# Squares of seven chunks added on GpSimd, and one visit of TensorE in place of seven, in three projections

## The reference, cut to what matters

```python
def rmsnorm(x, g):                       # first block: of x + g1 * y_lat, ahead of the second mixture of experts
    xf = x.astype(jnp.float32)
    y = xf * lax.rsqrt(jnp.mean(xf * xf, axis=-1, keepdims=True) + EPS)
    return (y * g.astype(jnp.float32)).astype(x.dtype)
...
m = stick_breaking_attention(hn, ...)    # ends with  o @ w_o   (1024 x 1024)
x = x + rms_norm(m, norm_gains[0, 1])
...
m = dilated_attention(hn, ...)           # ends with  o @ w_o   (512 x 1024)
x = x + rms_norm(m, norm_gains[1, 1])
```

## Time and profile before

| | |
|---|---|
| median of 3 runs | 2281.8 us (2281.36 to 2284.24) |
| span of the profiled execution | 2283.8 us |
| own time of the profiled execution | no other time is given for it than its span |
| PE busy | 2138.7 us (94%) |
| DVE busy | 1295.8 us (57%) |
| ACT busy | 1031.5 us (45%) |
| POOL busy | 133.7 us (6%) |
| mean granted TensorE clock | 0.973 of full speed |

### The profile page before, as it was taken

The page is one execution under the profiler, slowest core; times in us unless marked ns, Lnnn a source line. Parts: engine busy times, 40 slices in busy tenths (PEclk is TensorE's granted clock), DMA queues, the critical chain, the costliest instruction groups (busy, mean ns, idle before and its releaser), DMA issues.

```text
span 2283.8 us, 31295 instructions
## 1 busy us (share of the span) xinstructions
PE 2138.7 (94%) x13216; PEld 1640.1 (72%) x13216; DVE 1295.8 (57%) x1837; ACT 1031.5 (45%) x1501; POOL 133.7 (6%) x112
## 2 busy tenths in 40 slices
PE   5979989999997998999889999998999998999997
PEld 4656654577765665777667888886877776888885
DVE  3567765666637775355536766435255546766533
ACT  3556641255625664377744433324333355433331
POOL 0011200000001210000010000003000002000000
PEclk9989999999997998999999999999999999999998
DMA  9999970022217984211012222221222112222210
GB/s 398 384 361 370 369 298 0 17 95 112 112 75 263 357 343 187 111 38 38 38 74 111 105 80 111 92 110 52 91 95 95 48 71 78 111 77 108 111 56 37
DMA packets 40571, 324.12 MB, mean 142 GB/s; under 512 B 7231, under 2 KB 8255, under 8 KB 21695
## 3 DMA queue, kind: packets, MB, share of 16 engines
q1 hardware_dynamic: 27288, 288.91, 32.8%
q0 software_dynamic: 10624, 25.71, 3.2%
q10 hardware_dynamic: 2512, 7.41, 0.8%
HBM read 310.40 MB, written 24.19 MB: 147 GB/s over the span
## 4 chain that ended last, share of the span: by engine, by line
PE 85%; DVE 7%; ACT 4%; DMA 2%; issue 2%; POOL 0%; SPq 0%; DVEq 0%; ACTq 0%; POOLq 0%
PE PS L163 80%; PE PS L891 2%; PE PS L641 1%; DVE work L2344 1%; ACT work L1591 1%; DMA work<-tokens,slots 1%; PE PS L1152 1%; DVE WR L2350 1%; ACT XH L1284 0%; ACT work L1596 0%; ACT L1596 0%; DMA work<-in_xtok 0%; ACT work L1587 0%; DVE work L2405 0%; DMA ring<-in_wexp 0%
## 5 line engine op out<-in xcount | busy, mean ns | idle before, releaser
L163 PE MATMUL PS<-HS,RS 128*128 128x512 f32 x4128 | 951.0, 391 | 9.4 <-DVE HS L2121 8.6
L163 PEld LDWEIGHTS PS<-HS,RS 128*128 128x128 f32 x4128 | 773.8, 188 | 175.3 <-issue 13.7
L1765 DVE TENSOR_TENSOR RS<-ring,RS 128x1024 fp32r<-128x1024 f32 x212 | 259.0, 1224 | 342.2 <-ACT RS L1248 342.2
L1248 ACT ACTIVATE RS<-ring 128x1024 fp32r<-128x1024 f32 x212 | 221.5, 1052 | 252.3 <-PE PS L163 252.3
L1688 ACT ACTIVATE work<-work,vec 128x512 f32<-128x512 f32 x88 | 71.9, 817 | 239.5 <-DVE work L2471 239.5
L1765 DVE TENSOR_TENSOR CR<-ring,WR 128x1024 fp32r<-128x1024 f32 x128 | 153.3, 1222 | 37.5 <-ACT WR L1248 35.0
L163 PE MATMUL PS<-work 128*64 128x128 f32 (+5 forms) x1728 | 131.9, 294 | 29.7 <-DVE work L1824 19.9
L1248 ACT ACTIVATE WR<-ring 128x1024 fp32r<-128x1024 f32 x128 | 134.8, 1058 | 51.3 <-PE PS L163 44.9
L163 PEld LDWEIGHTS PS<-work 128*64 128x64 f32 (+2 forms) x1728 | 107.7, 147 | 49.4 <-issue 31.0
L1248 ACT ACTIVATE work<-PS 128x384 f32<-128x384 f32 (+2 forms) x194 | 86.7, 484 | 116.2 <-PE PS L674 37.4
L163 PE MATMUL PS<-RS,HS 128*128 128x512 f32 x480 | 116.0, 400 | 8.3 <-DVE HS L2121 8.3
(11 more groups left out here) (256 smaller groups left out, 2793.1 us busy)
## 6 DMA issues: line engine op xcount, KB each, us to landing
ring<-in_wexp SPq DMA_DIRECT2D x32, 2048.0 KB, 10.6
ring<-in_wmod SPq DMA_DIRECT2D x24, 2048.0 KB, 11.2
ring<-in_ffnu SPq DMA_DIRECT2D x22, 2048.0 KB, 8.1
ring<-in_wexp SPq DMA_DIRECT2D x32, 1024.0 KB, 11.0
ring<-in_ffnd SPq DMA_DIRECT2D x10, 2048.0 KB, 7.2
ring<-in_dilqk SPq DMA_DIRECT2D x6, 2048.0 KB, 8.1
ring<-in_sbqk SPq DMA_DIRECT2D x4, 2048.0 KB, 8.0
ring<-in_dilv SPq DMA_DIRECT2D x3, 2048.0 KB, 8.0
```

What stands on the lines that cost most here:

```text
L163: return T.matmul(out, l, r, start=start, stop=stop, skip_group_check=True)
L1248: return S.activation(out, x, ACT.Copy, **kw)
L1765: V.tensor_tensor(lo, src, hi.bitcast(F32), ALU.subtract).then_inc(w_lo, 1)
```

## The change

In calls 6, 8 and 12, ScalarE writes the square of chunk 0 to slot 0 of `sq`, those of chunks 1 to 7 in turn to slots 1, 2, 3 (`summed_square`, `summed_slot`). GpSimd adds the squares of chunks 1 to 6 to slot 0, one 128x512 add for each (`sum_squares`, semaphore `st_sum`). TensorE no longer visits the squares between the chunks: behind chunk 7's products `stat_sum` multiplies slot 0, once its six adds are done, and then the square of chunk 7. ScalarE waits with the square of chunks 4 to 7 for the add that read its slot before. `sum_squares(6)` is put ahead of `moe(1, 4)` in GpSimd's queue, `sum_squares(8)` ahead of the first `add_normed`, `sum_squares(12)` behind the fetches. The semaphore of the Abs is merged into that of the Exp.

```diff
--- before.py
+++ after.py
@@ -175,7 +175,8 @@
     ld_tab, tab_out, out_done = sem("landed_tables"), sem("tables_stored"), sem("out_stored")
     sc_ready = sem("sc_ready")
     ad_rows, ad_copy, ad_turn, ad_mod, ad_aff, ad_q = [sem("ada_" + n) for n in ("rows", "copied", "turned", "mod", "affine", "quarter")]
-    sq_act, sq_dve, st_add, st_sqrt, st_rcp, st_bc = [sem("stat_" + n) for n in ("sq_act", "sq_dve", "added", "sqrt", "rcp", "spread")]
+    sq_act, sq_dve, st_add, st_sum, st_sqrt, st_rcp, st_bc = [sem("stat_" + n) for n in (
+        "sq_act", "sq_dve", "added", "summed", "sqrt", "rcp", "spread")]
     md_a, md_b = sem("mod_scaled"), sem("mod_shifted")
     pl_mm, pl_ma, pl_md, pl_y, pl_x = [sem("pool_" + n) for n in ("means", "means_act", "means_dve", "product", "x")]
     rt_lg, rt_lt, rt_tr, rt_exp, rt_m, rt_rk, rt_blk = [sem("route_" + n) for n in ("logits", "biased", "turned", "exp", "chosen", "rank", "blocks")]
@@ -200,8 +201,8 @@
     nm_h, nm_l, rb_c, rc_c = sem("rows_hi"), sem("rows_lo"), sem("stat_row_copied"), sem("stat_column")
     pr_c, po_c = sem("rows_copied"), sem("out_copied")
     an_t, an_xp, an_xd = sem("add_scaled"), sem("add_pool"), sem("add_dve")
-    sk_q, sk_k, sk_z, sk_aa, sk_ad, sk_e, sk_ln, sk_s, sk_h, sk_l, sk_c, sk_t, sk_v = [sem("stick_" + n) for n in (
-        "q", "k", "z", "abs_act", "abs_dve", "exp", "log", "sum", "hi", "lo", "cumulated", "a", "values")]
+    sk_q, sk_k, sk_z, sk_ad, sk_e, sk_ln, sk_s, sk_h, sk_l, sk_c, sk_t, sk_v = [sem("stick_" + n) for n in (
+        "q", "k", "z", "abs_dve", "abs_exp", "log", "sum", "hi", "lo", "cumulated", "a", "values")]
     dq, dk, dz = sem("dil_q"), sem("dil_k"), [sem(f"dil_bias{i}") for i in range(3)]
     fu_r, fu_a, fu_d, fu_s, fu_f, fx_h, fx_l, fd_ca = [sem("ffn_" + n) for n in ("scaled", "tap2", "taps", "silu", "f", "f_hi", "f_lo", "copied_act")]
     po_half, own = sem("out_chunk"), sem("dve_step")
@@ -223,6 +224,11 @@
                 else:
                     na += 1
                     SQ[call, c] = (sq_act, na)
+    SUMMED = (6, 8, 12)
+
+    def summed_slot(c):
+        return (c - 1) % 3 + 1 if c else 0
+
     MD = (0, 16, 32, 48)
     BEFORE = [max([k for k in range(i) if CALLS[k][0] == CALLS[i][0]], default=-1) for i in range(len(CALLS))]
 
@@ -478,6 +484,16 @@
             for j in range(n // 128):
                 x = mm(PS[32 * j:32 * j + 32, s, 0:128], C("mean"), sq[:, i, j * 128:(j + 1) * 128], c == 0, c == 7)
             x.then_inc(st_add, 1)
+
+        def stat_sum(call):
+
+            s, n, both = CALLS[call]
+            for c, ready in ((0, (st_sum, 6 * SUMMED.index(call) + 6)), (7, SQ[call, 7])):
+                pe.wait_ge(*ready)
+                for j in range(n // 128):
+                    x = mm(PS[32 * j:32 * j + 32, s, 0:128], C("mean"), sq[:, summed_slot(c), j * 128:(j + 1) * 128],
+                           c == 0, c == 7)
+            x.then_inc(st_add, 8)
 
         def stat_spread(call):
             s, n, both = CALLS[call]
@@ -945,9 +961,7 @@
                     pe.wait_ge(f_l, k + 1)
                     x = mm3(PS[:, 4 + c % 2, :], (hi[:, k, :], lo[:, k, :]), hs(k), k == 0, k == 7)
                 x.then_inc(w_done, 1)
-                if c:
-                    stat_add(6, c - 1)
-            stat_add(6, 7)
+            stat_sum(6)
             stat_spread(6)
 
         def spread_sums(p, b, rl, at):
@@ -1010,9 +1024,7 @@
                 pe.wait_ge(po_c, po + c - 1)
                 x = out_products(first, kc, src_of, base, c, banks[c], range(0 if c else made, kc))
                 x.then_inc(w_done if c % per == per - 1 else po_half, 1)
-                if c:
-                    stat_add(call, c - 1)
-            stat_add(call, 7)
+            stat_sum(call)
             stat_spread(call)
 
         def stick():
@@ -1266,6 +1278,12 @@
             act.wait_ge(ready, value)
             S.activation(sq[:, SEQ[call, c] % 4, 0:x.shape[-1]], x, ACT.Square).then_inc(sq_act, 1)
 
+        def summed_square(call, c, x):
+            act.wait_ge(st_add, SEQ[call, 0])
+            if c > 3:
+                act.wait_ge(st_sum, 6 * SUMMED.index(call) + c - 3)
+            S.activation(sq[:, summed_slot(c), 0:x.shape[-1]], x, ACT.Square).then_inc(sq_act, 1)
+
         def table(s):
             S.activation(tiny[:, s:s + 1], C("eps"), ACT.Sqrt)
 
@@ -1519,7 +1537,8 @@
             act.wait_ge(sm_s, 64)
             for c in range(8):
                 split_hi("wo", ahead("wo", c))
-                square(6, c, XL[:, c, :], wo_x, c + 1)
+                act.wait_ge(wo_x, c + 1)
+                summed_square(6, c, XL[:, c, :])
             root(6)
 
         def sums_copied(p, b, rl, at):
@@ -1561,7 +1580,7 @@
                     act.wait_ge(w_done, first + c // per + 1)
                 else:
                     act.wait_ge(po_half, 7 + c // per + 1)
-                square(call, c, PS[:, banks[c], :], st_add, SEQ[call, c] - 3)
+                summed_square(call, c, PS[:, banks[c], :])
                 copy(HL[:, c, :], PS[:, banks[c], :]).then_inc(po_c, 1)
                 if c == 6:
                     split_hi(after, part_of[after].start + 2)
@@ -1584,15 +1603,15 @@
                     if h == 0:
                         act.wait_ge(sk_z, 2 * j + 1)
                         act.wait_ge(sk_c, 2 * (j - 1) + 1)
-                        S.activation(s_, zz[0], ACT.Abs).then_inc(sk_aa, 1)
-                        act.wait_ge(sk_aa, j + 1)
+                        S.activation(s_, zz[0], ACT.Abs).then_inc(sk_e, 1)
+                        act.wait_ge(sk_e, 3 * j + 1)
                     else:
                         act.wait_ge(sk_ad, j + 1)
                     S.activation(s_, s_, ACT.Exp, scale=-1.0).then_inc(sk_e, 1)
 
             def softplus(j):
                 for h in range(2):
-                    act.wait_ge(sk_e, 2 * j + h + 1)
+                    act.wait_ge(sk_e, 3 * j + h + 2)
                     S.activation(Sp[h][:, 128:1408], Sp[h][:, 128:1408], ACT.Ln, bias=1.0).then_inc(sk_ln, 1)
                 for h in range(2):
                     act.wait_ge(sk_s, 2 * j + h + 1)
@@ -2575,6 +2594,13 @@
             over(0)
             G.sem_inc(ov_over, 1)
 
+        def sum_squares(call):
+            done = 6 * SUMMED.index(call)
+            for c in range(1, 7):
+                pool.wait_ge(*SQ[call, c])
+                pool.wait_ge(st_sum, done + c - 1)
+                G.tensor_tensor(sq[:, 0, :], sq[:, 0, :], sq[:, summed_slot(c), :], ALU.add).then_inc(st_sum, 1)
+
         def add_normed(a):
             for n in range(0, 8, 1 if a < 3 else 2):
                 c = ORDER[a + 1][n] if a < 3 else n
@@ -2596,11 +2622,14 @@
                 G.dma_start(z[i % 3], src).then_inc(dz[i % 3], 16)
 
         moe(0, 6)
+        sum_squares(6)
         moe(1, 4)
+        sum_squares(8)
         add_normed(0)
         add_normed(1)
         for i in range(8):
             fetch(i)
+        sum_squares(12)
         add_normed(2)
         add_normed(3)
```

## The result

The changed kernel took 2272.16 us in the median of 4 runs (2268.66 to 2276.57), the kernel before 2282.01 us beside it (4 runs, 2281.36 to 2284.24). The ratio is 0.9954, 95% interval 0.9942 to 0.9966. The profiled execution took 2276.57 us and spans 2275.1 us, 8.7 less than that of before.

A forecast was written before the change was run, and what follows sets the result against it. TensorE, busy 94% of the span, was taken as the bound. Visits removed, 10.2 us, less 0.2 for ScalarE in dil gave 10.0, so 2281.8 - 10.0 = 2271.8 us, range 2270.0 to 2276.4 us.

The forecast's parts named there:

- TensorE bounds the three places: In wo, stick and dil TensorE is busy throughout, so an instruction taken from its queue saves its slot in time.
- a visit costs 0.56 to 0.57 us beyond the products: Chunk period less the products' own steps: 0.57 us per visit in wo, 0.56 in stick, 0.57 in dil.
- Six visits per call: Six visits between chunks go in each of wo, stick and dil: 10.2 us saved, bounds 6.3 and 10.8.
- The adds are hidden: 18 GpSimd adds of 1.26 to 2.11 us lie beside TensorE's products: price 0, bounds 0 and 0.2 us.
- ScalarE late in dil: ScalarE's work takes 2.98 us against 2.73 for TensorE, so the square comes 0.25 late: 0.2 us lost, or 0.1.
- VectorE's subtractions and the reciprocal in dil just fit: In dil two subtractions end 4.42 us behind chunk 6's square, reciprocal due at 4.5: price 0, bounds 0 and 0.7.
- rival 1: Wo, stick, dil: longer steps belong to the bank change and stay; saving 6.3 - 0.2, 2275.7 us; chance 0.06.
- rival 2: Dil: VectorE and GpSimd collide; reciprocal 0.7 us late, sum 0.2 at most; saving 9.1, 2272.7 us; chance 0.08.
- rival 3: Second mixture of experts hangs on a transfer, not wo's end; wo's 3.4 us lost, 2275.2 us; chance 0.05.
- rivals 4 and 5: Dil: chained adds late from 2.6 us each, 2272 to 2282 us, chance 0.07; at 5.1 slower, 2286.6 us, chance 0.04.

The follow-up runs named there:

- Dil alone: The change made in dil only, wo and stick visited as in the kernel before: 2280.45 us against 2283.68, ratio 0.9982.
- The pairs: The kernel before, with its visits in wo, stick and dil taken two at a stop, three stops fewer per call: 2283.30 us, ratio 0.9994.
- the two repetitions: The changed kernel run again unchanged, against the kernel before: 2273.62 us, ratio 0.9952, and 2272.85 us, ratio 0.9956.

## Why the prediction was right, point by point

- *TensorE bounds the three places* and *a visit costs 0.56 to 0.57 us beyond the products*: periods of 5.46, 5.56 and 2.73 us were forecast, 5.44, 5.57 and 2.72 measured. Without adds, and with the adds on VectorE, the saving stays; what these programs share is that TensorE's visits are gone. Dil alone gave dil's share.
- *Six visits per call*: 3.5, 3.3 and 3.4 us, in all 10.2 us with ScalarE's lateness in dil already taken off; the sum had 10.0 for that.
- *The adds are hidden*: shown by leaving them out. An add took 1.29 us, at the low end of what was taken, and TensorE did not wait for the sum.
- *ScalarE late in dil*: it is, by 0.15 us, not 0.25; its next square starts before the record of the split ahead of it ends (1879.12 against 1877.23 + 2.01 = 1879.24), which the prediction had as a possibility, at 0.1. Dil saved 3.38 us where 3.2 was forecast.
- *VectorE's subtractions and the reciprocal in dil just fit*: the reciprocal starts at 1880.66, in the moment in which the subtractions end (1878.32 + 2.36 = 1880.68), 0.89 us behind the second visit as before (1889.57 - 1888.67 = 0.90).
- *The gaps stay* (rival 1): refuted by the periods. The pairs show that the gaps belong to the stop and go with it.
- *Collision in dil* (rival 2): it does not occur, by 0.1 us: the add ends at 1878.23, the subtraction starts at 1878.32, and all 18 adds take 1.28 to 1.30 us. (The prediction counted the add from the last product and the subtraction from the square 0.1 us behind it; with one origin the same rows give this gap.) In wo the two do meet; VectorE's subtraction takes 1.48 us there for 1.23, with nobody waiting. The Trainium skill ("SBUF — State Buffer", Terms) has the shared ports held for a whole instruction while the loser stands fully still. The adds made two and three times fit this in kind: a subtraction of 1.22 us delays GpSimd by 0.9 to 0.97 us, somewhat less than its whole length.
- *Something behind wo does not move* (rival 3): the first two profiles looked like a part of it (+1.68 and +1.14 us against before), the third did not (-1.69). The 3.4 us of wo are not lost as a whole, since the medians differ by 9.0 to 10.9 us in the three series; a loss of a microsecond is not excluded.
- *GpSimd late* (rivals 4 and 5): the place was right, and adds made three times do turn the gain into a loss. The threshold was mis-sized. I put it at 2.6 us of adds per chunk; two adds, 2 x 1.29 = 2.58 by their records, already cost TensorE a wait of 4.40 us, since back to back they step by 1.36 and collide with VectorE.
- The total: 10.0 us forecast, 2282.01 - 2272.16 = 9.9 measured; 2271.8 against 2272.16 us. That the two agree to 0.4 us is in part luck: the interval of the ratio stands for a saving of 7.8 to 13.2 us, and the changed kernel's medians in the two repetitions are 2273.62 and 2272.85. What the runs bear out more firmly is the mechanism, by the periods and the three stretches.

## What to carry to other kernels

A small product between streams of large ones can cost more than its recorded duration (here 0.57 us for 0.43): read the period of the loop with and without it, then see whether an engine that the stretch leaves idle can sum in its place. Taking several at one stop saved 0.35 us per stop in the timeline, but nothing that the medians showed. Before giving the idle engine more, compare the period with its work at the back-to-back step, collisions with its neighbour included: two adds with a record of 1.29 us each seemed to fit into 2.72 us and did not. For a change of 0.5% compare the stretches that it touches in the traces, since a stretch that it does not touch differed by 3.4 us between profiles of the same program (247.62 and 244.25).

## What the runs showed of the hardware

Between equal instructions, many of the small differences go with TensorE's granted clock. Behind wo, the same spread of the reciprocal took 1.78 us in the profile of before and 1.17 in that of after. The windows of TensorE that answer to this, before and then after, show the granted clock ahead of and behind that point:

```profile
676.00:679.00 3.00, 1.76 (x8) 0.76 1.01 431
679.00:682.00 3.00, 1.32 (x20) 0.50 0.97 412
```

```profile
673.00:676.00 3.00, 1.16 (x8) 0.95 1.02 437
676.00:679.00 3.00, 2.58 (x34) 0.50 0.97 412
```

In both TensorE has just waited twice for ScalarE and VectorE, 1.2 and 1.5 us long, and the clock goes from full to half. Before, it falls during the spread, which starts at 677.20: it is 1.00 from there to 677.50 and 0.50 from 678.00 to 678.50. After, the spread runs from 673.53 to 674.70 at 1.00, and the clock falls behind it. The dilated attention, whose instructions no program changed, took 288.06 to 290.32 us in the profiles named here.

GpSimd and VectorE hold each other up where both work from SBUF: a subtraction of 1.22 us delays a stream of GpSimd's adds by 0.9 to 0.97 us, and is itself recorded with 1.47 to 2.36 us. Adds of GpSimd that each wait for the one before start 1.36 us apart, though each is recorded with 1.29.
